# All low parts on GpSimd in turns with the one-hots, twelve more dots among the groups of each layer, and loads, shift products and square sums in another order

## What is computed

```python
c_act = silu(c)
for l in range(2):
    mod = c_act @ mod_w[l] + mod_b[l]                      # 6 vectors: shift, scale, gate, twice
    h = rms_norm(x, norm1_g[l]) * (1 + sc1) + sh1
    y = conv_gmlp_mixer(h) if l == 0 else short_conv_mixer(h)
    x = x + g1 * y
    h = rms_norm(x, norm2_g[l]) * (1 + sc2) + sh2
    x = x + g2 * peer(h, pk_wq[l], pk_subkeys[l], pk_u[l], pk_v[l])
return rms_norm(x, final_g)

def peer(h, wq, subkeys, u_tab, v_tab):     # 8 heads, 16 of 16384 experts per head and position
    ... e, gate = product-key top 16 of q = h @ wq; gate = softmax(best)
    act = gelu(sum_d u_tab[e] * h)
    return sum_k (gate * act)[k] * v_tab[e[k]]
```

## Time and profile before

| | us |
|---|---|
| three runs | 3013.38, 3016.1, 3016.72 (median 3016.1) |
| profiled execution | 3017.65, its span 3015.9 |
| PE busy | 2870.5 (95%) |
| DVE, ACT, POOL busy | 2373.0, 1208.8, 1216.5 |

### The profile page before, as it was taken

One profiled execution on the slowest core, in us unless ns is written; L12 is line 12 of the kernel. 1 busy time (PEld: TensorE's weight loads), 2 busy tenths in 40 slices (PEclk: granted clock), 3 DMA queues, 4 the chain that ended last, 5 costly groups with the idle time before them and its releaser, 6 DMA issues.

```text
span 3015.9 us, 47979 instructions
## 1 busy us (share of the span) xinstructions
PE 2870.5 (95%) x15754; PEld 2545.4 (84%) x15754; DVE 2373.0 (79%) x4326; ACT 1208.8 (40%) x1590; POOL 1216.5 (40%) x788
## 2 busy tenths in 40 slices
PE   4978999999997999999999899999999979999998
PEld 3756899999997888888878689999999968888886
DVE  7965699989994788888855316999999848888887
ACT  2433333446663333333332334333566523333333
POOL 2623378873336122222224334878533442222220
PEclk8989999999999999999999999999999989999999
DMA  6335678889999999999934224888899999999995
GB/s 249 140 119 198 223 241 280 268 302 326 336 348 385 319 354 352 354 353 353 351 127 172 79 70 149 281 274 277 291 349 342 338 352 356 353 352 353 356 354 207
DMA packets 364590, 850.71 MB, mean 282 GB/s; under 512 B 31392, under 2 KB 195360, under 8 KB 363808
## 3 DMA queue, kind: packets, MB, share of 16 engines
q1 hardware_dynamic: 239888, 479.53, 46.4%
q0 software_dynamic: 73728, 268.47, 24.7%
q10 hardware_dynamic: 50832, 100.84, 8.7%
HBM read 741.76 MB, written 106.95 MB: 281 GB/s over the span
## 4 chain that ended last, share of the span: by engine, by line
PE 89%; DVE 6%; DMA 3%; ACT 1%; issue 0%; SPq 0%; POOL 0%; ACTq 0%; DVEq 0%
PE bank L1457 12%; PE bank L1458 12%; PE bank L1459 12%; PE bank L1407 11%; PE bank L1409 11%; PE bank L1408 11%; PE bank L1428 4%; PE bank L1307 4%; PE bank L1309 4%; PE bank L1308 4%; DVE rows L1207 3%; DMA w_raw<-stream 1%; PE bank L1385 1%; PE bank L1351 1%; PE bank L1323 1%; PE bank L1324 1%
## 5 line engine op out<-in xcount | busy, mean ns | idle before, releaser
L549 ACT ACTIVATE w_hi<-w_raw 128x1024 fp32r<-128x1024 f32 x342 | 361.9, 1059 | 706.4 <-PE bank L1459 666.3
L1457 PE MATMUL bank<-w_hi,h_hi 128*128 128x512 f32 x1536 | 600.3, 391 | 32.4 <-DVE h_lo L1080 32.4
L1458 PE MATMUL bank<-w_hi,h_lo 128*128 128x512 f32 x1536 | 599.9, 391 | 0.0
L1459 PE MATMUL bank<-w_lo,h_hi 128*128 128x512 f32 x1536 | 599.5, 390 | 0.0
L491 POOL DMA_INDIRECT shared<-stream,v_idx x256 | 241.0, 941 | 806.0 <-DVE rows L1123 738.1
L1086 DVE TENSOR_TENSOR w_lo<-w_raw,w_hi 128x1024 fp32r<-128x1024 f32 x256 | 313.7, 1225 | 201.6 <-ACT w_hi L549 201.6
L1407 PE MATMUL bank<-h_hi,w_hi 128*128 128x384 f32 x1376 | 465.7, 338 | 3.1 <-ACT act_words L627 3.1
L1409 PE MATMUL bank<-h_lo,w_hi 128*128 128x384 f32 x1376 | 460.1, 334 | 0.0
L1408 PE MATMUL bank<-h_hi,w_lo 128*128 128x384 f32 x1376 | 459.9, 334 | 0.0
L1457 PEld LDWEIGHTS bank<-w_hi,h_hi 128*128 128x128 f32 x1536 | 289.6, 189 | 93.2 <-issue 32.9
L1459 PEld LDWEIGHTS bank<-w_lo,h_hi 128*128 128x128 f32 x1536 | 289.7, 189 | 60.5
(11 more groups left out here) (203 smaller groups left out, 5277.6 us busy)
## 6 DMA issues: line engine op xcount, KB each, us to landing
w_raw<-stream SPq DMA_DIRECT2D x600, 512.0 KB, 5.3
act_dram<-act_words ACTq DMA_DIRECT2D x256, 192.0 KB, 4.7
gate_dram<-shared ACTq DMA_DIRECT2D x96, 512.0 KB, 7.0
shared<-act_dram SPq DMA_DIRECT2D x256, 192.0 KB, 5.6
shared<-gate_dram SPq DMA_DIRECT2D x128, 384.0 KB, 6.1
oh_j<-mod_rows SPq DMA_DIRECT2D x60, 512.0 KB, 5.4
oh_ic<-mod_rows SPq DMA_DIRECT2D x20, 512.0 KB, 5.7
shared<-mod_rows SPq DMA_DIRECT2D x16, 512.0 KB, 14.0
```

What stands on the lines that cost most here:

```text
L549: nc.scalar.activation(hi_of(grp, s), w_raw[:, s, :], ACT.Copy).then_inc(S["hi_ready"], 1)
L1457: MM(o, p_hi, hi, start=start, stop=False)
L1458: MM(o, p_lo, hi, start=False, stop=False)
L1459: ins = MM(o, p_hi, lo, start=False, stop=stop)
```

## The change

It does seven things. (1) SP loads the first two weight tiles between the 8 scale tiles and the 8 shift tiles of `mod_w`; POOL makes no low part before DVE has made the roots of norm 0 (`diag_ready`). (2) `c_row` is copied to `rows`, which lies in PSUM, and the row sums at the start multiply by that copy. (3) The shift vectors 2 to 4 of layer 0 come from PE, 24 products of a 128x128 block with one column of silu(c), from `mod_w` tiles that are stored in another layout; DVE takes two row sums ahead of the multiplications of x and three behind them. (4) In both residual norms DVE adds up blocks 1 to 6 of the squares into block 0 (`add_square`), and PE sums blocks 0 and 7 with eight products whose moving side is one column; the result is one column for each 128 positions, so `take_diagonal` isn't needed there. (5) POOL makes all low parts of the U pass; for tiles 70 to 115 it first waits until the one-hots of the group before are made. (6) `dots_to` gives one more dot for every second group in place of every fourth: 118 of the 128 dots by the end of the groups, 12 more for each layer. (7) From U to V: SP loads V tile 0 ahead of the wait for the gates, V tile 1 behind the first pair of the products' inputs and tiles 2 and 3 behind the second; ACT evacuates U tile 126 before it makes the high part of V tile 0, and makes the first product's high part ahead of the Gelu of the dots.

```diff
 def dots_to(g):
-    return EARLY + g + (g + 3) // 4 + (BESIDE if g > 1 else 0)
+    return EARLY + g + (g + 1) // 2 + (BESIDE if g > 1 else 0)
-GROUP_LOWS = range(GROUP_TILE + 4, GROUP_TILE + 1 + GROUPS)
...
         def _(sp):
             for i in range(MOD_A):
+                if i == KC:
+                    for s in range(2):
+                        sp.dma_start(w_raw[:, s, :], stream[s]).then_inc(ld[s], 16)
...
                 for s in range(RING):
                     load(first - 1, s)
+                load(first, 0)
                 for r in range(2):
                     sp.wait_ge(g_st[r], GATE_STORED * ((l + 1) * DB + 1))
                 for s in range(RING):
                     sp.wait_ge(act_st[s], 16 * (l * EXPERT_TILES // RING + 1))
                     load_products(0, s)
-                for s in range(RING):
-                    load(first, s)
+                    if s % 2:
+                        load(first, s // 2 + 1)
+                load(first, RING - 1)
...
         def _(pool):
+            pool.wait_ge(S["diag_ready"], 1)
             for s in range(RING):
                 make_lo(0, s)
...
                 for j in range(EXPERT_TILES):
-                    if j not in GROUP_LOWS:
-                        pool.wait_ge(S["hi_ready"], first + j + 1)
-                        if j == GROUP_LOWS.stop:
-                            pool.wait_ge(S["lo_ready"], first + j)
-                        nc.gpsimd.tensor_tensor(u_lo(j), w_raw[:, j % RING, :], u_hi(j).bitcast(F32), ALU.subtract
-                                                ).then_inc(S["lo_ready"], 1)
+                    pool.wait_ge(S["hi_ready"], first + j + 1)
+                    if GROUP_TILE + 2 <= j < GROUP_TILE + GROUPS:
+                        pool.wait_ge(S["oh_ready"], l * GROUPS + j - GROUP_TILE)
+                    nc.gpsimd.tensor_tensor(u_lo(j), w_raw[:, j % RING, :], u_hi(j).bitcast(F32), ALU.subtract
+                                            ).then_inc(S["lo_ready"], 1)
...
         def _(act):
+                def first_prod_hi():
+                    prod_hi(0, 0, True)
+                    act.wait_ge(S["dot"], (l + 1) * SLOTS)
+                    nc.scalar.activation(dots[:], dots[:], ACT.Gelu).then_inc(S["dot_act"], 1)
...
                     if j + 3 < EXPERT_TILES:
                         u_high(j + 3)
-                    elif j >= EXPERT_TILES - 2:
-                        make_hi(v_first, j - (EXPERT_TILES - 2))
...
                     act.dma_start(act_dram[j], act_ring[:, s, :]).then_inc(act_st[s], 16)
+                    if j >= EXPERT_TILES - 2:
+                        make_hi(v_first, j - (EXPERT_TILES - 2))
+                        if j == EXPERT_TILES - 2:
+                            first_prod_hi()
...
             nc.scalar.activation(c_row[:], c_row[:], ACT.Silu).then_inc(S["c_ready"], 1)
+            act.wait_ge(S["c_ready"], 1)
+            nc.scalar.copy(rows[:], c_row[:]).then_inc(S["c_rows"], 1)
             act.wait_ge(S["inputs"], 16 * N_INPUTS)
+            nc.scalar.activation(c_col[:], cols[:, COLS["c"]:COLS["c"] + KC], ACT.Silu).then_inc(S["c_col_ready"], 1)
...
         def _(dve):
             def norm_root(n):
                 dve.wait_ge(S["ssum"], n + 1)
-                link(take_diagonal(0, 5, D))
-                inverse_roots(1)
+                if n in RESIDUAL:
+                    inverse_roots(1, ps[5][:, 0:TB])
+                else:
+                    link(take_diagonal(0, 5, D))
+                    inverse_roots(1)
...
                     V.tensor_tensor(x[:, k, :], x[:, k, :], y_slot[:, k % 2, :], ALU.add).then_inc(S["x_ready"], 1)
+                    if k >= 2:
+                        add_square(n, k - 1)
+            def add_square(n, k):
+                had = RESIDUAL.index(n) * (KC - 2)
+                dve.wait_ge(S["sq_ready"], n * KC + k + 1)
+                if k > 1:
+                    dve.wait_ge(S["sq_sum"], had + k - 1)
+                V.tensor_tensor(sq[:, 0, :], sq[:, 0, :], sq[:, k, :], ALU.add).then_inc(S["sq_sum"], 1)
...
                 for g in range(GROUPS):
                     one_hots(g)
-                    j = GROUP_TILE + 1 + g
-                    if j in GROUP_LOWS:
...
-                        V.tensor_tensor(u_lo(j), w_raw[:, j % RING, :], u_hi(j).bitcast(F32), ALU.subtract
-                                        ).then_inc(S["lo_ready"], 1)
                     for n in range(dots_to(g), dots_to(g + 1)):
                         dot(n)
...
-                mod_row_sum(mod_a_ring[:, i % MOD_A_RING, :], c_row[:], mod[:, m:m + 1]).then_inc(S["mod_a_done"], 1)
+                mod_row_sum(mod_a_ring[:, i % MOD_A_RING, :], rows[:], mod[:, m:m + 1]).then_inc(S["mod_a_done"], 1)
...
-            mod_a(KC)
+            for m in range(PE_MODS.start):
+                mod_a(KC + m)
...
-            for i in range(KC + 1, 2 * KC):
-                mod_a(i)
-            dve.wait_ge(S["mod_a_done"], MOD_A)
-            add_bias(0, KC, mod[:, 0:KC])
+            for m in range(PE_MODS.stop, KC):
+                mod_a(KC + m)
+            dve.wait_ge(S["mod_a_done"], MOD_A - N_PE_MODS)
+            add_bias(0, PE_MODS.start, mod[:, 0:PE_MODS.start])
+            add_bias(PE_MODS.stop, KC - PE_MODS.stop, mod[:, PE_MODS.stop:KC])
+            dve.wait_ge(S["shift_mm"], N_PE_MODS)
+            add_bias(PE_MODS.start, N_PE_MODS, ps[4][:, 0:N_PE_MODS])
...
         def _(pe):
-                for k in range(2, KC + 2):
-                    if k < KC:
-                        project(g + k // RING, k % RING, b + k)
-                    square_sum(n, k - 2)
+                for k in range(2, KC):
+                    project(g + k // RING, k % RING, b + k)
+                pe.wait_ge(S["sq_sum"], (RESIDUAL.index(n) + 1) * (KC - 2))
+                pe.wait_ge(S["sq_ready"], (n + 1) * KC)
+                for b in range(TB):
+                    for k in (0, KC - 1):
+                        ins = MM(ps[5][:, b:b + 1], sq[:, k, b * P:(b + 1) * P], ones[:, 0:1], start=(k == 0), stop=(k > 0))
+                ins.then_inc(S["ssum"], 1)
+                spread_roots(ROOTS_BEFORE[n], 5)
...
             sum_squares(0)
+            pe.wait_ge(S["c_col_ready"], 1)
+            for n in range(N_PE_MODS):
+                i = KC + PE_MODS.start + n
+                pe.wait_ge(mod_a_ld[i % MOD_A_RING], 16 * (i // MOD_A_RING + 1))
+                for k in range(KC):
+                    ins = MM(ps[4][:, n:n + 1], mod_a_ring[:, i % MOD_A_RING, k * P:(k + 1) * P], c_col[:, k:k + 1],
+                             start=(k == 0), stop=(k == KC - 1))
+                ins.then_inc(S["shift_mm"], 1)
```

56 lines of the change are left out of this document (27 added, 29 removed).

## The result

The changed kernel takes 3020.57 us (median of 22 runs, 3014.53 to 3027.49), the kernel before in the same runs 3016.47 (22 runs). The ratio is 1.0015, 95% interval 1.0009 to 1.0022: a little slower, by less than the 0.2% that was called no change, where 54.5 us less were forecast. The profiled execution of after is a short one of its kind (3017.16 us, span 3015.4), so the two profiles differ by 0.5 us.

The account below looks back on a forecast made before the run. PE was taken to bound the groups, DVE close behind, with PE's holes from U to V, at the start and in the norms. Start 10.5, turn 39, groups 0, norms 5 sum to 54.5: 3016.1 to 2961.6 us, range 2953 to 2986.

Parts of the forecast that it names:

- The start: Up to PE's first product with weights: fewer and faster row sums gain 10.5 us, bounds 7.3 and 11.4.
- POOL's new wait for the roots costs nothing: At the start: POOL's lows are wanted at 38 us and two of them take under 7, so cost 0.
- The turn: From U to V, both layers: PE's holes of 15.6 and 16.7 us close; gain 39 us, bounds 15.5 and 40.8.
- I leave 0.9 for each layer: From U to V: allowance for V tile 4, loaded only when U tile 127's store has landed, beside eight V row fetches.
- the margin of 5 us for the first inputs: From U to V: products' inputs land by about 955, while ACT needs the first product near 959 to 961.
- The first rival: From U to V: half the hole stays, through late gate pieces or late V tile 4; 2982 us, chance 0.14.
- The groups: The 48 groups of each layer: PE stays the bound at 5.6 us a group, so the change there is 0.
- The low part begins when the one-hots end and must end before the next begin, 5.6 - 2.93 = 2.7 later, which 2.33 does: In the groups: POOL's low part of 2.33 us fits between DVE's one-hots without meeting them.
- The price of a hit (2.16): In the groups: one-hots beside a POOL low part take 5.09 us against 2.93, so 2.16 for each collision.
- the second rival: In the groups: POOL, late by a second fetch, collides with DVE's one-hots; 99 us slower than forecast, 3061, chance 0.05.
- the ring: In the groups, a follow-up theory: POOL's low part holds the one-hots, the next waits for these; cycles 5.4 or 6.1 us.
- The norms: The two residual norms: fewer square sums on PE between tiles, 2.5 us each; gain 5, bounds 1 and 9.6.

Follow-up runs that it names:

- no_turns_late_hold: The change without POOL's wait for the one-hots, V tiles 4 to 7 loaded sooner, V rows fetched only after U tile 127's evacuation: 2983.04 us, ratio 0.9885.
- no_turns_timed: The change without POOL's wait for the one-hots in the groups, nothing else changed: 2982.68 us, ratio 0.992.
- lows_undone: The change with the low parts of the groups back on DVE, new number of dots kept: 2987.36 us, ratio 0.9904.

## Why the prediction was wrong

**The start: right in kind, 10.5 against 7.9 at the first product.** Four sums fewer, all at 1.2 us with the second input in PSUM, and narrow products that hide, as said: 48 records in 10.24 us, 0.213 each, between the two rates that were weighed, over at 37.6 and 1.4 us ahead of the last sum. The step that failed is "POOL's new wait for the roots costs nothing". It made POOL's low part begin 0.02 us ahead of DVE's gain, which then took 2.35 us in place of 0.17, 2.2 of the 2.6 that are missing. PE's lower clock level also lasted until 46.4 us (granted clock 0.68 from 40 to 50 us), 5.9 behind the first product where it was 3.0 before, so the 0.4 added for it weren't there.

**The turn: right in mechanism, 39 against 16.** The hole closed, with V tile 0 and its inputs in time. Of layer 0's 20.1 us, 7.8 went in waits for V tiles 1 and 4, some 2.2 in products at the lower level behind the second of them (eleven, at 0.43 and more in place of 0.23), and 2.2 in the tail of U, where four tiles took 4.77 in place of 4.16, the time of a low part and two fetches on POOL: 7.9 are left, 7.2 were measured. The step that failed is "I leave 0.9 for each layer" for tile 4. It was priced as a delay, but it is a chain of its own: evacuation of tile 127, its store beside eight V row fetches, SP's wait for all stores, then tile and inputs, 17.2 us of SP's waiting. The step before it was half wrong too: the last gate piece still landed 19.1 us after its issue (941.42, SP goes on at 960.50), against a median of 20.8 for the last two, in spite of fewer fetches beside them; the margin of 5 us for the first inputs was in truth none, DVE made the first products at 966.88. The first rival gave the turn half of its hole and named both causes; its 2982 is near what the changed kernel without the loss in the groups runs at.

**The groups: the step that decided, 0 against -28.6.** The step that failed is "The low part begins when the one-hots end and must end before the next begin, 5.6 - 2.93 = 2.7 later, which 2.33 does". This takes DVE as paced by PE. DVE isn't: it runs ahead until its own work stops it, and after one dot it begins the next compare 1.15 us later. Then "behind it are only its own fetches, and they land in 7.3 us": those that DVE waited for landed 5.1 to 10.9 us after their issue, about as said, but the issue was late, and DVE waited 28.8 us for them. And the sum for POOL, 4.2 to 5.5 a group, holds for its work (10.43 for two groups) but lacked the time that the wait itself makes, 1.11 in each second turn. The price of a hit (2.16) was near enough for a held compare (1.3 to 2.1); the second rival named a loss that is real. A low part that is late behind a second fetch and holds the compare is half of the ring (730.47 and 730.98 above), and without the wait it took 27 us in one layer of no_turns_late_hold, where some 50 were put on it. But it was given 0.05 on the strength of the wait, and the wait itself was given no price: no rival had that. Its count of hits was off too. In no_turns_timed nearly every compare is held, 0.9 us on average, and PE loses 0.4 us a layer, where by the rival four hits in ten groups were to be the limit.

**DVE's own time** in a group before was read as 5.6. In lows_undone two groups with two low parts, three dots and two one-hots take 11.55; with half a dot less, as before, that is (11.55 - 0.57) / 2 = 5.5 (an estimate from 1.14 a dot). The reading was 0.1 too long and decided nothing.

**The norms: 5 against 2.3.** Each square sum less between tiles was true, but DVE's additions, both inputs in SBUF, fell beside POOL's low parts. Timeline of DVE in after, the end of `ev_out` (L890 adds to x, L900 is `add_square`):

```profile
207.42 2.72 DVE L900 TENSOR_TENSOR shared<-shared 128x512 f32<-128x512 f32 x1
...
212.95 2.88 DVE L900 TENSOR_TENSOR shared<-shared 128x512 f32<-128x512 f32 x1
...
218.03 2.74 DVE L890 TENSOR_TENSOR x<-x,shared 128x512 f32<-128x512 f32 x1
```

They take 0.68 alone. I had counted that for the last one (2 us) and not for all before. In norm 1 DVE also has two row sums to a tile, so it became the pace there: PE's tiles came 5.44 apart and its last wait for the squares grew from 1.4 to 5.4 us (232.4). Nothing was left.
